# A hybrid mLSTM, attention and expert layer on one core: projection jobs alternate by kind, gate weights stand side by side, and the expert unit 0 and the final rows are split by halves

## The reference, cut to what matters

```
hn = rmsnorm(x, norm_mix);  z = hn @ w_in + b_in            # 2824 columns
mq, mk, mv, mo, mi, mf, aq, ak, av = split(z)               # 512 x4, 4, 4, 512, 128, 128
mq, mk = silu(causal_conv4(mq)), silu(causal_conv4(mk))     # 4 taps along the tokens
hm = mlstm_chunkwise(mq, mk, mv, mi, mf)                    # 4 heads of 128, input and forget gates
hm = sigmoid(mo) * rmsnorm_per_head(hm) * mlstm_norm
ha = windowed attention with sinks and relative bias (aq, ak, av)   # 8 heads of 64, 2 kv heads
x  = x + concat(hm, ha) @ w_out
xt = rmsnorm(x, norm_ffn)
group = argmax(xt @ w_grp + b_grp);  e1, e2 = top2 of (xt @ w_er + b_er) inside the group
x  = x + sum over e1, e2 of gate_e * (silu(xt @ w_gate[e]) * (xt @ w_up[e])) @ w_down[e]
out = rmsnorm(x, norm_final)
```

## Time and profile before

| | |
|---|---|
| median of 3 runs | 1008.14 us (1007.99 to 1009.78) |
| the profiled execution, its own time | 1007.17 us |
| its span in the trace | 1005.3 us |
| busy: PE, PEld | 949.1 us (94%), 783.8 us (78%) |
| busy: DVE, ACT, POOL | 652.7 us (65%), 444.6 us (44%), 265.0 us (26%) |
| share of PE in the chain that ended last | 77% |
| matmuls | 5090 |
| moved by DMA | 184.05 MB, mean 183 GB/s |

### The profile page before, as it was taken

One profiled execution on the slowest core, in us unless ns is written; L12 is line 12 of the kernel. 1 busy time (PEld: TensorE's weight loads), 2 busy tenths in 40 slices (PEclk: granted clock), 3 DMA queues, 4 the chain that ended last, 5 costly groups with the idle time before them and its releaser, 6 DMA issues.

```text
span 1005.3 us, 15833 instructions
## 1 busy us (share of the span) xinstructions
PE 949.1 (94%) x5090; PEld 783.8 (78%) x5091; DVE 652.7 (65%) x1103; ACT 444.6 (44%) x701; POOL 265.0 (26%) x292
## 2 busy tenths in 40 slices
PE   7999999999999899999849999999999999999896
PEld 5788777778999778888737778888887788778674
DVE  6662587875444896677588896565556565586556
ACT  6512344332333442222226775445446555474653
POOL 1300000000000010000026875323416644474434
PEclk9999999999999999999859999999999999999998
DMA  8441111101203832225358999688678895898775
GB/s 287 100 124 42 42 42 43 42 16 59 85 22 126 266 132 75 89 80 187 123 210 300 371 361 378 210 268 251 190 248 241 256 339 170 289 298 278 198 245 239
DMA packets 86308, 184.05 MB, mean 183 GB/s; under 512 B 8379, under 2 KB 29200, under 8 KB 86258
## 3 DMA queue, kind: packets, MB, share of 16 engines
q1 hardware_dynamic: 76114, 153.48, 43.9%
q0 software_dynamic: 9984, 29.84, 11.5%
q10 hardware_dynamic: 160, 0.07, 0.0%
HBM read 151.41 MB, written 31.40 MB: 182 GB/s over the span
## 4 chain that ended last, share of the span: by engine, by line
PE 77%; DVE 10%; DMA 4%; issue 3%; ACT 3%; POOL 1%; SPq 0%; DVEq 0%; POOLq 0%; ACTq 0%
PE PS L1773 22%; PE PS L1775 21%; PE PS L1774 21%; PE PS L2056 2%; DVE WL L1583 1%; DVE WP L577 1%; PE PS L2038 1%; DMA XT<-in_x_dram 1%; DMA xn_dram<-xnb 1%; DMA comb_dram<-comb 1%; PE PS L1903 1%; PE PS L1917 1%; PE PS L2023 1%; PE PS L1877 1%; PE PS L1780 1%
## 5 line engine op out<-in xcount | busy, mean ns | idle before, releaser
L1583 DVE TENSOR_TENSOR WL<-RAW,WH 128x2048 fp32r<-128x2048 f32 x94 | 214.2, 2291 | 93.5 <-ACT WH L1034 91.0
L1034 ACT ACTIVATE WH<-RAW 128x2048 fp32r<-128x2048 f32 x96 | 183.9, 1915 | 28.8 <-PE PS L1775 17.9
L1773 PE MATMUL PS<-WH,XH 128*128 128x512 f32 x400 | 164.2, 410 | 5.6 <-issue 3.9
L1775 PE MATMUL PS<-WH,XL 128*128 128x512 f32 x400 | 157.2, 393 | 0.0
L1774 PE MATMUL PS<-WL,XH 128*128 128x512 f32 x400 | 156.8, 392 | 0.0
L792 POOL TENSOR_TENSOR dst<-dst,stat 128x4 f32<-128x4 f32 x8 | 8.2, 1020 | 338.2 <-DVE dst L1546 338.2
L1773 PEld LDWEIGHTS PS<-WH,XH 128*128 128x128 f32 x400 | 75.6, 189 | 23.8 <-issue 10.4
L800 POOL TENSOR_TENSOR stat<-stat 128x1 f32<-128x1 f32 x92 | 67.9, 746 | 96.9 <-ACT YB L1120 78.7
L1775 PEld LDWEIGHTS PS<-WH,XL 128*128 128x128 f32 x400 | 75.5, 189 | 16.8
L1773 PE MATMUL PS<-HNH,WP 128*128 128x512 f32 x208 | 85.0, 409 | 1.6 <-issue 1.6
L1774 PEld LDWEIGHTS PS<-WL,XH 128*128 128x128 f32 x400 | 75.8, 190 | 13.5
(11 more groups left out here) (356 smaller groups left out, 1868.1 us busy)
## 6 DMA issues: line engine op xcount, KB each, us to landing
RAW<-in_w_gate_dram SPq DMA_DIRECT2D x32, 1024.0 KB, 9.8
RAW<-in_w_up_dram SPq DMA_DIRECT2D x32, 1024.0 KB, 10.7
RAW<-in_w_down_dram SPq DMA_DIRECT2D x32, 1024.0 KB, 5.0
wraw<-in_w_in_dram SPq DMA_DIRECT2D x22, 512.0 KB, 4.1
XT<-in_x_dram SPq DMA_DIRECT2D x8, 512.0 KB, 7.4
vo_dram<-vo SPq DMA_DIRECT2D x16, 256.0 KB, 2.1
wout<-in_w_out_dram SPq DMA_DIRECT2D x4, 1024.0 KB, 7.1
VM<-vo_dram SPq DMA_DIRECT2D x16, 256.0 KB, 5.5
```

The source lines that it names most:

```text
L1034: A(WH[:, d % SPLITS, :], RAW[:, j, :], ACT.Copy).then_inc(s_whi, 1)
L1583: V.tensor_tensor(WLS[d % SPLITS][:, :], RAW[:, TURN[d][1] if d else 0, :], WH[:, d % SPLITS, :].bitcast(fp32), ALU.subtract).then_inc(s_w ...
L1773: mm(bank, ah, bh, start=start, stop=False)
L1775: return mm(bank, al, bh, start=False, stop=stop)
```

## The change

Eight edits are made together.

1. The gate job's stationary operand holds high and low parts side by side (128 columns), so 2 matmuls replace 3 in each chunk. Its first half waits for 4 of the 8 token tiles, its weights are split ahead of the last tile, and its eviction takes 4 operations for a half, where 2 were, and adds the parts afterwards. Four matmuls on constants stand ahead of it.
2. The 32 slots alternate: two row jobs, then two token jobs. `pre` has 1 buffer (before 2), `vo` has 2 (before 4). Convolutions fall in slots 1, 5, ..., 29; weight groups are split in slots 5, 7, 13, 15, 21 and 23. The load of the first two 1 MB pieces of `w_out` moves two slots later.
3. In step 8 `top2(5)` comes ahead of `normed_rows(6)`.
4. PE gets 4 matmuls on constants within the routing tables and 9 behind them.
5. `comb_dram` is stored ahead of the wait for the tables.
6. Unit 0's second half is transposed and split only where it is filled, and PE waits for its first half's gather alone. The value that tells this is loaded ahead of the transposes.
7. POOL's drain moves from the end to the last full unit, and two variances are computed ahead of the last splits.
8. In the last unit PE takes the second row half through both pieces first and adds its rows afterwards; the first half's rows are added by DVE in SBUF (`add_rows` for that half is gone), its squares and scaling follow the last token tile.

The diff, cut to its core:

```
         SLOT0 = len(JOBS)
-        JOBS += [("mk", h, t) for h in range(H) for t in range(2)]
-        JOBS += [("mq", h, t) for h in range(H) for t in range(2)]
-        JOBS += [("mv", g, i) for g in range(2) for i in range(4)]
-        JOBS += [("mo", g, i) for g in range(2) for i in range(4)]
+        for rows_kind, tokens_kind in (("mk", "mv"), ("mq", "mo")):
+            for g in range(2):
+                for half in range(2):
+                    JOBS += [(rows_kind, 2 * g + half, t) for t in range(2)]
+                    JOBS += [(tokens_kind, g, 2 * half + t) for t in range(2)]
         NJ = len(JOBS)
 
...
-        GROUPS = [C_AK, C_AQ, C_AQ + 256, 512, 768, 0, 256, C_MV, C_MV + 256, C_MV + 512, C_MV + 768]
+        GROUPS = [C_AK, C_AQ, C_AQ + 256, 512, C_MV, 768, C_MV + 256, 0, C_MV + 512, 256, C_MV + 768]
         NG = len(GROUPS)
-        GROUP_OF = {"ak": lambda a: 0, "av": lambda a: 0, "aq": lambda a: 1 + a // 2, "mk": lambda a: 3 + a // 2,
-                    "mq": lambda a: 5 + a // 2, "mv": lambda a: 7 + a, "mo": lambda a: 9 + a}
+        GROUP_OF = {"ak": lambda a: 0, "av": lambda a: 0, "aq": lambda a: 1 + a // 2, "mk": lambda a: 3 + a // 2 * 2,
+                    "mq": lambda a: 7 + a // 2 * 2, "mv": lambda a: 4 + 2 * a, "mo": lambda a: 8 + 2 * a}
...
+        VO_SLOTS = [j for j in range(32) if j % 4 >= 2]
+        SILU_SLOTS = [j for j in range(32) if j % 4 == 2]
+        GATE_SLOTS = [VO_SLOTS[m] + 1 for m in range(8, 16)]
...
+                    for m in range(2 * g - 10, 2 * g - 8):
                         store_vo(sp, m)
             w_out_v = w_out.rearrange("(k p) n -> p k n", p=P)
-            for m in range(4, 13):
-                if m == 11:
-                    sp.wait_ge(s_job, LAST_JOB[NG - 2] + 1)
-                    for h in range(2):
-                        sp.dma_start(wout[:, 4 + 2 * h:6 + 2 * h, :],
-                                     w_out_v[:, 4 + 2 * h:6 + 2 * h, :]).then_inc(s_w[h], 16)
+            for m in range(12, 14):
                 store_vo(sp, m)
+            sp.wait_ge(s_job, LAST_JOB[NG - 2] + 1)
+            for h in range(2):
+                sp.dma_start(wout[:, 4 + 2 * h:6 + 2 * h, :],
+                             w_out_v[:, 4 + 2 * h:6 + 2 * h, :]).then_inc(s_w[h], 16)
 
...
             store_xn(sp, NT - 1)
             store_acc(sp, NT - 2)
             store_acc(sp, NT - 1)
+            sp.wait_ge(s_cmb, 1)
+            sp.dma_start(comb_dram.rearrange("(t p e) o -> p t (e o)", p=P, e=NE), comb[:, :, :]).then_inc(s_cmbst, 16)
             sp.wait_ge(s_tab, 1)
             n_loop = sp.value_load(tab[0:1, 3 * NU:3 * NU + 1], min_val=NE - 2, max_val=MAXU - 1)
             sp.wait_ge(s_wlo, 1)
             load_piece(0, sp.value_load(tab[0:1, 1:2], min_val=0, max_val=NE - 1))
-            sp.wait_ge(s_cmb, 1)
-            sp.dma_start(comb_dram.rearrange("(t p e) o -> p t (e o)", p=P, e=NE), comb[:, :, :]).then_inc(s_cmbst, 16)
...
             gather_half(0, idx, 0)
-            gather_half(1, idx, 0)
+            nc.gpsimd.indirect_dma_start(
+                XGS[0][:, 1, :], None, xn_dram, bass.IndirectOffsetOnAxis(ap=idx[:, 1:2], axis=0)
+            ).then_inc(s_sink, 16)
             pool.wait_ge(s_acc, 16 * NT)
             pool.wait_ge(s_xn, NT)
             pool.wait_ge(s_tab, 1)
             gather(1, 1, 1)
-            gather_half(1, idxcs[1], 1)
+            second = pool.value_load(tab[0:1, 1 + NU:2 + NU], min_val=0, max_val=1)
+            with pool.If(second > 0):
+                gather_half(1, idxcs[1], 1)
+            with pool.If(second < 1):
+                pool.dma_start(XGS[1][0:1, 1, :], xn_dram[0:1, :]).then_inc(s_gath[1], 16)
...
+                if not more:
+                    pool.drain()
...
                 ).then_inc(s_gath[0], 16)
-            pool.drain()
...
                     A(nmc, PS[:, 6, 0:KD], ACT.Copy).then_inc(s_nmc, 1)
-            act.wait_ge(s_wgn, 1)
-            act.wait_ge(s_set, 3)
-            A(gate_cols(0), wg8_if, ACT.Copy).then_inc(s_wgh, 1)
+                if i == NT - 2:
+                    act.wait_ge(s_wgn, 1)
+                    act.wait_ge(s_set, 3)
+                    A(gate_cols(0), wg8_if, ACT.Copy).then_inc(s_wgh, 1)
             act.wait_ge(s_nmc, 1)
             group_hi(act, 0)
...
-                V.tensor_tensor(rowI[:, half], PS[0:H, n % 4, :], rows_of(t)[0:H, :], ALU.mult)
-                V.tensor_tensor(rowF[:, half], PS[32:32 + H, n % 4, :], rows_of(t)[32:32 + H, :],
-                                ALU.mult).then_inc(s_evd, 1)
+                for at_, row in ((0, rowI), (32, rowF), (64, rowB), (96, rowM)):
+                    last = V.tensor_tensor(row[:, half], PS[at_:at_ + H, n % 4, :], rows_of(t)[at_:at_ + H, :], ALU.mult)
+                last.then_inc(s_evd, 1)
             dve.wait_ge(*emptied(n))
-            V.tensor_scalar(rowI[:, :], rowI[:, :], gbias[:, 0:1], None, ALU.add)
-            link(V.tensor_scalar(rowF[:, :], rowF[:, :], gbias[:, 1:2], None, ALU.add))
+            V.scalar_tensor_tensor(rowI[:, :], rowI[:, :], gbias[:, 0:1], rowB[:, :], ALU.add, ALU.add)
+            link(V.scalar_tensor_tensor(rowF[:, :], rowF[:, :], gbias[:, 1:2], rowM[:, :], ALU.add, ALU.add))
...
                                     ALU.mult).then_inc(s_hh, 1)
-                if 2 <= s < NT + 1:
+                if 2 <= s < NT:
                     normed_rows(s - 2)
                 if s >= 3:
                     top2(s - 3)
+                if s == NT:
+                    normed_rows(s - 2)
                 if 1 <= s <= NT:
...
+            def variance(c):
+                dve.wait_ge(s_f2a, c + 1)
+                V.tensor_scalar(var_of(c), sum_of(c), 1.0 / D, EPS, ALU.mult, ALU.add).then_inc(s_fv, 1)
+
+            variance(0)
+            variance(1)
...
             dve.wait_ge(s_nfin, 16)
-            variance(0)
-            for c in range(NT):
-                if c + 1 < NT:
-                    variance(c + 1)
+            for c in range(NT - 1):
+                if c + 2 < NT:
+                    variance(c + 2)
                 scale(c, tile_of(c))
-            for n, hf in enumerate((1, 0)):
-                variance(NT + n)
-                dve.wait_ge(s_f3, NT + n + 1)
-                V.scalar_tensor_tensor(halves(rows_[:, hf, :]), last_rows(hf), rstd_of(NT + n), halves(nfin),
-                                       ALU.mult, ALU.mult).then_inc(s_f4, 1)
+            variance(NT)
+            dve.wait_ge(s_gath[0], 16 * n_loop + 64 - FEWER[0])
+            for half in range(2):
+                cols_ = slice(512 * half, 512 * half + 512)
+                dve.wait_ge(s_wused, 6 * u + 5 + half + SPLITS)
+                V.tensor_tensor(rows_[:, 0, cols_], PS[:, 4 + half, :], rows_[:, 0, cols_], ALU.add).then_inc(s_fz, 1)
+            scale(NT - 1, last_tile[:, :])
+            dve.wait_ge(s_f2a, NT + 2)
+            link(V.tensor_scalar(sum_of(NT + 1), fin[:, 30:31], EPS * D, None, ALU.add))
+            dve.wait_ge(s_f2a, NT + 3)
+            V.tensor_scalar(var_of(NT + 1), fin[:, 31:32], sum_of(NT + 1), 1.0 / D, ALU.add, ALU.mult).then_inc(s_fv, 1)
+            dve.wait_ge(s_f3, NT + 1)
+            V.scalar_tensor_tensor(halves(rows_[:, 1, :]), PS[:, 1:4:2, :], rstd_of(NT), halves(nfin),
+                                   ALU.mult, ALU.mult).then_inc(s_f4, 1)
+            scale(NT + 1, rows_[:, 0, :])
 
...
                 elif kind == "gates":
-                    pe.wait_ge(*emptied(2 * NT - 1))
+                    pe.wait_ge(*emptied(NT * b + NT - 1))
                     pe.wait_ge(s_wgl, 2)
                     tok = slice(512 * b, 512 * b + 512)
                     for k in range(KD):
-                        last = split3(bank[0:32 + H, :], wgs[:, k, 0, 0:32 + H], wgs[:, k, 1, 0:32 + H],
-                                      HNH[:, k, tok], HNL[:, k, tok], k == 0, k == KD - 1)
+                        both_parts = wgs[:, k, :, :].rearrange("p a b -> p (a b)")
+                        mm(bank, both_parts, HNH[:, k, tok], start=(k == 0), stop=False)
+                        last = mm(bank, both_parts, HNL[:, k, tok], start=False, stop=(k == KD - 1))
                 else:
                     g = GROUP_OF[kind](a)
...
                     tr(PS[:, 6, 0:KD], nmr[:, :], ident[0:KD, 0:KD]).then_inc(s_nmt, 1)
+            for _ in range(4):
+                mm(PS[:, 7, 0:P], ones[:, :], ones[:, :], start=True, stop=True)
...
+            def keep_busy(n):
+                for _ in range(n):
+                    mm(PS[:, 5, 0:P], ones[:, :], ident, start=True, stop=True)
+
+            keep_busy(4)
             pe.wait_ge(s_uni, 2)
             mm(PS[:, 2, 8:8 + 3 * NU + 1], ones[0:NE, :], acu[:, :], start=True, stop=True).then_inc(s_cnt, 1)
...
 
-            pe.wait_ge(s_gath[0], 32)
-            x_group(0, 0)
-            x_group(1, 0)
+            keep_busy(9)
             pe.wait_ge(s_tab, 1)
```

(40 more changed lines are left out.)

135 lines of the change are left out of this document (68 added, 67 removed).

## The result

The changed kernel took 996.94 us (median of 4 runs, 992.59 to 998.58) against 1008.3 (1007.99 to 1009.78): a ratio of 0.9878, 95% interval 0.9843 to 0.9912. The forecast was 992.2. Both sets are of one kernel, so two profiles of it are read here: the first (998.58 us, span 996.8) and the second (990.34, span 988.5).

A forecast was written before the change was run, and what follows sets the result against it. PE was taken as the bound, busy 949.1 of 1005.3 us. Gains of 3.3 + 2.4 + 5.5 + 3.6 + 1.1 = 15.9 from 1007.17, plus 0.97, gave 992.2 us; its own range was 988 to 998, stated range 985 to 1000.

The forecast's parts named there:

- Opening: Gate job up to the value jobs: squares hold the row factor, value jobs start at 40.7; gain 3.3 us (2.3 to 3.8).
- Slots: The 32 slots: three PE stalls of 2.2 us instead of four, plus clock, less w_out's delay; gain 2.4 us.
- The clock term: In the slots: three idle stretches with the same odds of a clock fall cost 2.2 us, not 2.9; gain 0.7.
- rival (c): Slots: with two vo buffers, evictions wait for stores queued behind loads on SP; slower, 1030 us; chance 0.04.
- Step 8: top2(5) first: PE's wait of 3.08 us goes, and 2.4 of low clock; gain 5.5 us (3.1 to 6).
- no wait of line 1968: Sign that the forecast is right: PE no longer waits at this line; no size of its own.
- Tables and unit 0: Routing tables to unit 0: earlier first product, higher clock, halved transposes, earlier combine weights; gain 3.6 us (1.5 to 5).
- The 0.9 for the combine weights: Unit 0: combine weights issued at 517.9 land by 526.2, so the 0.86 wait passed to PE goes; 0.9 us gained.
- End: Last unit: PE's row additions and DVE's scaling finish earlier, last tile by 1.85 us; gain 1.1 us (0 to 1.9).
- (d): Rival, whole kernel: clock gains nothing; step 8 keeps 3.1, entry 2.3, end 0.4, slots lose 1.5; 1001 us; chance 0.08.
- (a): Rival, slots: all stalls vanish as DVE's work is spread; 983.5 us; chance 0.12.
- (b): Rival, expert weights: PE starts early, then waits for the weight stream, losing about 5 us; 997.5 us; chance 0.13.

The follow-up runs named there:

- the two sets: Changed kernel against the kernel before, measured twice: 996.94 us, ratio 0.9878, first; then 991.18 us, ratio 0.9807, in a later set.
- The fillers: Changed kernel plus 12 matmuls on constants between the first key job and the wait for rdiag: 990.52 us, ratio 0.9809 to the kernel before.

## Why the prediction was right, and where not

The whole came out as forecast, between the two sets (12.3 and 19.5 us by their ratios, 15.9 forecast), the terms less so. That it fits so well is partly luck. The opening fell short by 2.6 to 4.3 us and the slots gave 0.7 to 3.7 more than forecast, and which of the two sets is nearer hangs on falls that nobody forecast one by one.

**Opening: the failed step.** "PE can issue line 1839 at 33.65" was right (33.41), and so was what holds it, the squares. The idle time "for 1.4 us" was 2.87: the gate products start at 16.56 and the key job at 24.73, 6.7 us earlier than before, not 5.5. And nothing was allowed for what that idle stretch does: the clock fell behind it in all five profiles that have this stretch of idle time (2.76 to 2.87 us), so the rdiag matmuls took up to 3.78 instead of 1.88 and the value jobs came at 43.8 or 42.0 instead of 40.7. The prediction charged a fall to stalls of 2.2 us in the slots, but not to one that it had itself put into the opening. The fillers remove it.

**Slots: right in kind, too small.** Three stalls, by the rule that a convolution and low parts stand in one slot. Each is 1.97 long, not 2.2, so 8.7 became 5.9, 2.8 gained. The clock term was the mis-sized one: 0.7 at "the same odds" was 0 in the first profile, which has two falls as before, and 3.2 in the others, which have none. Stalls of 2.1 to 2.2 us were followed by a fall 10 times of 20 (five profiles), those of 1.97 twice of 27 (nine profiles). The 0.5 for w_out didn't show: in the second profile the slots are shorter by 6.05, and 2.8 and two falls of 1.6 fill it. The store of vo, rival (c), waited nowhere.

**Step 8** gave 4.5 and 6.1 for 5.5: the wait of 3.08 went and the clock stayed up; the first profile has a fall at 480 that the second lacks. The prediction's sign "no wait of line 1968" failed, though: the next bound came in view sooner than it had it. The second rank's wait, 2.04 before, becomes 4.20 when PE comes without a fall. The DVE work that PE's 24 matmuls were to cover is not covered, and the chain to the tables is DVE's there.

**Tables and unit 0** gave 2.8 up to the first product where 1.5 was forecast, and 3.2 when tried alone (14.19 to 10.98); in both profiles the clock is up within 3 us of it. Of the 2.8, the transposes begin 0.7 earlier, take 0.9 less, and 1.2 less is idle between them and the product. The units then differ by 2.5 between the two profiles of this one kernel, so the 0.4 can't be told from the times. The 0.9 for the combine weights can be followed in DVE's timeline. The wait of 0.86 for the gates is gone in the first profile, but in the second it is 1.98: the gather now waits for its indices from DVE, no longer for the store, and takes 8.1 us, and behind it PE waits 0.99 for XL and 0.85 for HL. So this term moved the bound and is no sure gain (timeline of DVE, second profile):

```profile
524.90 0.75 DVE L1692 SCALAR_TENSOR_TENSOR HB<-HB,gt,PS 128x512 f32<-128x512 f32 x1 [1.98 <-DMA gt<-comb_dram,gix]
```

**End.** The 1.1 lies between -1.4 and 1.6. PE's side came as worked out in the second profile, within 0.7 us (the last matmul starts 15.1 us behind the last hidden transposes, where it was 18.8), and its last tile is scaled 1.6 us earlier, where 1.85 was forecast. Two things were missed. ACT's conversion stands behind two squares whose tiles are loaded from memory, and when the load is late, PE waits for HL (timelines of ACT and PE, first profile):

```profile
965.84 1.06 ACT L1173 ACTIVATE fjunk<-VM 128x1024 f32<-128x1024 f32 x1 [1.64 <-DMA VM<-acc_dram]
968.15 1.89 ACT L1049 ACTIVATE WH<-RAW 128x2048 fp32r<-128x2048 f32 x1
971.52 0.79 PE L1807 MATMUL PS<-WH,HH 128*128 128x512 f32 x1 [2.65 <-DVE HL L1682]
```

The tail behind the last matmul grew from 9.0 to 11.2 us, since two scalings stand between the additions and the last one; the prediction followed the last tile, not the scatter behind it (timelines of DVE and POOL, first profile):

```profile
986.03 0.69 DVE L1785 TENSOR_TENSOR XG<-PS,XG 128x512 f32<-128x512 f32 x1 [0.67 <-PE PS L1809]
986.64 1.27 DVE L1773 SCALAR_TENSOR_TENSOR last_tile<-last_tile,fin,VM 128x1024 f32<-128x1024 f32 x1
988.14 1.27 DVE L1792 SCALAR_TENSOR_TENSOR XG<-PS,fin,VM 128x1024 f32<-128x1024 f32 x1
989.34 1.27 DVE L1773 SCALAR_TENSOR_TENSOR XG<-XG,fin,VM 128x1024 f32<-128x1024 f32 x1
992.83 0.99 POOL L918 DMA_INDIRECT out_dram<-XG,idsc  x1 [0.30 <-issue]
```

Of the rivals, (d) described the first profile in part: the opening and the end gained nothing there through the clock. (a) and (b) are not in any trace: three stalls stay, and no wait of PE for RAW or of more than 0.6 us for WL is in the two profiles' tables. The rule on weight loads (Trainium skill, TensorE: Matmul & The Clock Gate, LDWEIGHTS) did not decide: the side-by-side gate products start 0.23 apart, 128 columns where there were 36. Their loads take 188 ns each and stay hidden behind the matmuls.

The 988 to 998 that the forecast had as its own range is about the spread of single runs of this one kernel, 989.97 to 998.58: falls of 1.6 us that come or don't make a large part of it. How much of the difference between the sets is the chip's is not shown.

## What to carry to other kernels

Before summing an edit's gain, list where it creates a new idle stretch on PE: the first matmuls behind it may run at half speed, and matmuls on constants that fill a short stretch cost nothing here while the wait lasted, though their gain of 2 to 3 us at the mark was not seen in the whole time. Compare stages by distances between equal instructions in several profiles; here, differences that came in equal amounts of 1.6 us were falls of the clock, not work. At an end, follow the last transfer to its last operand and move every operation that doesn't feed it out of that way.

## What was not expected of the hardware

The clock falls without any idle time, behind 3.1 us of matmuls of 4 rows or 20 columns in which PE counts as busy: 39 times of 48, and 0 of 4 when these stood between matmuls of 512 columns. It doesn't fall every time in the same program and place, and one fall costs 1.6 us. Two sets of runs differed by 0.7% in the ratio of the same two kernels (0.9878 and 0.9807, intervals apart), so kernels of different sets can't be compared here to better than that. The sets ran on different chips as far as the record names them, and whether it is the chip was not tried.
